# Moving the low parts of split f32 operands by 128 bytes in SBUF

## What is computed

```python
for l in range(2):                                   # first block
    z = rms_norm(x, norm_mix[l]) @ w_in[l]           # 1024 x 2560
    x = x + mix(z) @ w_out[l]                        # 1024 x 1024
    h = rms_norm(x, norm_mlp[l])
    x = x + square(relu(h @ w_mlp_in[l])) @ w_mlp_out[l]
for l in range(2):                                   # second block
    x = layer_norm(ALPHA * x + mix2(x, mem) @ w_out[l])
    h = einsum('td,thkd->thk', x, u[expert])         # u: 16384 x 1024
    x = layer_norm(ALPHA * x + einsum('thk,thkd->td', gelu(h) * gate, v[expert]))
```

## The kernel before

| tensor | before | after |
|---|---|---|
| `RAW`, `HI`, `HH`, `AH` | 128 | 128 |
| `LO`, `HL`, `AL` | 128 | 0 |
| `XH` | 64 | 64 |
| `XL` | 64 | 192 |
| `MEMH`, `MEML` | 128 | 0 |
| `G`, `RB`, `SQ`, `XS2`, first three `KVM` | 128 | 0 |

## Time and profile before

### The profile page before, as it was taken

How to read it: one execution, slowest core, us unless ns; L and a number is a source line. 1 busy time by engine, 2 the same in 40 slices (tenths; PEclk the granted TensorE clock), 3 DMA queues, 4 the chain that set the end, 5 groups by cost and what they waited for, 6 DMA issues and landing times.

```text
span 2731.0 us, 45677 instructions
## 1 busy us (share of the span) xinstructions
PE 2652.6 (97%) x18520; PEld 2418.1 (89%) x18520; DVE 1706.0 (62%) x2680; ACT 1373.5 (50%) x1713; POOL 191.1 (7%) x130
## 2 busy tenths in 40 slices
PE   8989999899999999999999999999999999999997
PEld 7869889699888999999999888988999999999886
DVE  5657446475455899655555666566899655555665
ACT  5555343654364569644444443444578634444442
POOL 0210000300001500000000000002400000000000
PEclk9999999999999999999999999999999999999999
DMA  5316552155535446756565675524356756556672
GB/s 219 109 66 218 197 204 94 62 204 199 189 113 194 152 165 237 278 202 225 203 215 206 240 267 194 189 78 156 140 181 242 280 195 224 207 211 219 227 268 86
DMA packets 74411, 515.99 MB, mean 189 GB/s; under 512 B 8272, under 2 KB 8544, under 8 KB 18592
## 3 DMA queue, kind: packets, MB, share of 16 engines
q1 hardware_dynamic: 58576, 424.70, 43.6%
q0 software_dynamic: 10208, 43.45, 4.5%
q10 hardware_dynamic: 5488, 45.91, 4.1%
HBM read 474.19 MB, written 39.85 MB: 188 GB/s over the span
## 4 chain that ended last, share of the span: by engine, by line
PE 87%; DVE 9%; ACT 2%; issue 1%; DMA 1%; POOL 1%; ACTq 0%; DVEq 0%; POOLq 0%
PE lin L1590 17%; PE lin L1592 17%; PE lin L1591 17%; PE m L1590 9%; PE m L1592 8%; PE m L1591 8%; PE m L2127 4%; DVE lo L958 1%; PE m L1709 1%; PE m L1730 1%; POOL w L1532 1%; PE m L2106 0%; PE m L2026 0%; PE lin L1764 0%; PE m L1742 0%
## 5 line engine op out<-in xcount | busy, mean ns | idle before, releaser
L958 DVE TENSOR_TENSOR lo<-raw,hi 128x2048 fp32r<-128x2048 f32 x357 | 817.8, 2296 | 652.9 <-ACT hi L448 651.8
L448 ACT ACTIVATE hi<-raw 128x2048 fp32r<-128x2048 f32 x403 | 769.7, 1913 | 479.8 <-PE m L1592 340.8
L1590 PE MATMUL lin<-xh,hi 128*128 128x256 f32 x3376 | 962.3, 285 | 16.2 <-DVE lo L958 9.0
L1591 PE MATMUL lin<-xl,hi 128*128 128x256 f32 x3376 | 943.3, 279 | 0.0
L1592 PE MATMUL lin<-xh,lo 128*128 128x256 f32 x3376 | 943.0, 279 | 0.0
L1590 PEld LDWEIGHTS lin<-xh,hi 128*128 128x128 f32 x3376 | 636.7, 189 | 24.9 <-DVE lo L958 10.2
L1592 PEld LDWEIGHTS lin<-xh,lo 128*128 128x128 f32 x3376 | 641.3, 190 | 0.0
L1591 PEld LDWEIGHTS lin<-xl,hi 128*128 128x128 f32 x3376 | 638.0, 189 | 3.6 <-issue 1.0
L1590 PE MATMUL m<-hi,ah 128*128 128x512 f32 x1024 | 398.8, 389 | 0.0
L1592 PE MATMUL m<-hi,al 128*128 128x512 f32 x1024 | 398.4, 389 | 0.0
L1591 PE MATMUL m<-lo,ah 128*128 128x512 f32 x1024 | 398.4, 389 | 0.0
(11 more groups left out here) (358 smaller groups left out, 2928.1 us busy)
## 6 DMA issues: line engine op xcount, KB each, us to landing
raw<-stream SPq DMA_DIRECT2D x403, 1024.0 KB, 4.8
gate_table<-stg ACTq DMA_DIRECT2D x16, 2048.0 KB, 10.9
g<-gate_table POOLq DMA_DIRECT2D x32, 1024.0 KB, 8.6
rows<-rows ACTq DMA_DIRECT2D x4, 1024.0 KB, 6.9
memh<-mem_turned_scratch POOLq DMA_DIRECT2D x3, 1024.0 KB, 5.1
meml<-mem_turned_scratch POOLq DMA_DIRECT2D x3, 1024.0 KB, 8.3
x_scratch<-x ACTq DMA_DIRECT2D x2, 1024.0 KB, 4.2
x<-x_scratch ACTq DMA_DIRECT2D x2, 1024.0 KB, 6.8
```

Source lines behind the costliest of these rows:

```text
L448: act.activation(HI[i % SLOTS][:], RAW[:, i % SLOTS, :], ACT.Copy).then_inc(hi_ready, 1)
L958: dve.tensor_tensor(LO[i % SLOTS][:], RAW[:, i % SLOTS, :], HI[i % SLOTS][:].bitcast(F32), ALU.subtract).then_inc(lo_ready, 1)
L1590: pe.matmul(out_, ah, bh, start=first, stop=False, **kw)
L1591: pe.matmul(out_, ah, bl, start=False, stop=False, **kw)
```

## The change

All low parts that take part in `three` are given a place 128 bytes off, modulo 256, from that of their high parts. For this `LOW = 128` is added ahead of `LO`, of `XL` and of `AL`, and to the offsets of `HL`; padding that stood in the cursor's way is lessened by the same amount, so that `XH` and `CST` and all behind them stay where they were. `MEMH` and `MEML` and some buffers that follow a shifted one move along. No instruction is added, removed or moved: on each engine the same instructions stand in the same order with the same waits, and only the addresses in them differ.

```diff
--- before.py
+++ after.py
@@ -14,6 +14,7 @@
 AX = mybir.AxisListType
 
 P = 128
+LOW = 128
 TOK = 256
 TT = TOK // P
 D = 1024
@@ -152,11 +153,12 @@
 
         RAW = at("raw", [P, SLOTS, HP])
         HI = [at(f"hi{i}", [P, HP], F32R) for i in range(SLOTS)]
+        cursor[0] += LOW
         LO = [at(f"lo{i}", [P, HP], F32R) for i in range(SLOTS)]
-        cursor[0] += 192
+        cursor[0] += 192 - LOW
         XH = at("xh", [P, KT, TOK], F32R)
+        cursor[0] += LOW
         XL = at("xl", [P, KT, TOK], F32R)
-        cursor[0] += 128
         cst0 = cursor[0]
         CST = at("cst", [P, N_CONST])
         SMALL = at("small", [P, 112])
@@ -198,16 +200,16 @@
         PM = at("pm", [P, 3, 2, TOK], off=r1)
         PT = at("pt", [P, 2, 2, TOK], off=r1 + 6144)
         MEMR = at("memr", [P, TT, D], off=mix0 + 8192)
-        MEMH = at("memh", [P, KT, TOK], F32R, off=mix0 + 40960)
-        MEML = at("meml", [P, KT, TOK], F32R, off=mix0 + 49152)
-        KVM = [at(f"kvm{i}", [P, 512], off=mix0 + (57344 if i < 3 else 8192)) for i in range(N_MEM)]
+        MEMH = at("memh", [P, KT, TOK], F32R, off=mix0 + 40960 + LOW)
+        MEML = at("meml", [P, KT, TOK], F32R, off=mix0 + 49152 + LOW)
+        KVM = [at(f"kvm{i}", [P, 512], off=mix0 + (57344 + LOW if i < 3 else 8192)) for i in range(N_MEM)]
 
         HH = at("hh", [P, 32, TOK], F32R, off=mix0)
-        HL = at("hl", [P, 32, TOK], F32R, off=mix0 + 32768)
-        RB = at("rb", [P, 2, 2 * TOK], off=mix0 + 65536)
-        SQ = at("sq", [P, 2 * TOK], off=mix0 + 65536 + 4096)
-        XS2 = at("xs2", [P, TT, D], off=mix0 + 65536)
-        assert mix0 + 65536 + 8192 <= top - 4 * LEVELS * 128
+        HL = at("hl", [P, 32, TOK], F32R, off=mix0 + 32768 + LOW)
+        RB = at("rb", [P, 2, 2 * TOK], off=mix0 + 65536 + LOW)
+        SQ = at("sq", [P, 2 * TOK], off=mix0 + 65536 + LOW + 4096)
+        XS2 = at("xs2", [P, TT, D], off=mix0 + 65536 + LOW)
+        assert mix0 + 65536 + LOW + 8192 <= top - 4 * LEVELS * 128
 
         def cst(name):
             a, b = CONST[name]
```

## The result

The changed kernel takes 2792.8 us (median of two runs, 2792.7 to 2792.9) against 2738.83: ratio 1.0185, 95% interval [1.0163, 1.0206]. It is slower. The forecast was 2736 with a range up to 2780; the result lies outside it and near rival C (2798).

A forecast was written before the change was run, and what follows sets the result against it. TensorE, 97% busy, was taken to bound the kernel through `three`'s products. Pairs 0 and `memh` -0.5 us took 2733.2 to 2732.7; with the runs' median 2738.8 and redrawn paces, 2736 was forecast, range 2706 to 2780.

The forecast's parts named there:

- rival C: TensorE triples: own weights or another neighbour's count, so two of three pairs change; 65 us slower, 2798; chance 0.11.
- every effect must be one of addresses: Whole kernel: the change moves no instruction, only start addresses, so only addresses can have an effect.
- The DVE row: DVE's low part `lo<-raw,hi`: expected within 20 ns of 2292; net cost taken as 0.
- and of no other: TensorE: only the next product's weights load beside a product, so only that pair's addresses can collide; the change keeps its distance.
- 3376 x 0 + 1280 x 0 = 0 us: Cost of the shifted pairs in 3376 triples of 256 columns and 1280 of 512: nothing, since each pair keeps its distance.
- this untested half: The claim that only the next product's weights matter, on which case A, no change in the pairs, rested; chance 0.76.
- 64 and 192 both occur now without harm at 256 columns: Argument against rival C: both distances modulo 256 between moving data and weights already occur in 256-column triples without harm.
- The two paces: 256-column triples run at 0.353 or 0.340 us; about 1650 of 3376 at the slow one, costing about 22 us.
- B: Rival: the slow pace of 256-column triples goes; 22 us faster (30 at the upper count), 2711; chance 0.08.
- If locks are drawn anew: 256-column stretches may lock into either pace afresh, 11 us either way, putting the next median between 2732.7 and 2738.8.
- D: Rival: the products' basic overhead goes at both widths; 80 us faster, 2653, or 104 us by the skill's formula, 2629; chance 0.05.
- a third pace: TensorE triples at a pace other than the known ones: listed as a sign of being wrong, without a price.

The follow-up runs named there:

- e7: The changed kernel with the second and third product of each triple exchanged, all addresses kept; ratio to the kernel before 1.0108, median 2772.1 us.
- m1: Kernel before, experts' product operands read beside their place in thirty-two settings, values wrong; only paces used: 256 columns 340 to 363 ns, 512 columns 680 to 701.
- W+X1: Setting in m1: product 3's weights and product 1's moving data 128 bytes further; 353 ns at 256 columns (base distance 192), 699 at 512 (base distance 0).
- e5: Kernel before with low parts 128 bytes further only for panels of 256-column triples, each low tile 128 bytes longer; ratio 0.9974, 2739.0 us beside 2745.4.

## Why the prediction was wrong, step by step

- "every effect must be one of addresses", and one of TensorE's products: right. The DVE row moved by 1 ns (forecast: within 20), no wait took a gap's place, `g`, `rb`, `sq`, `xs2` and `kvm` cost nothing that can be seen, and the products account for 57.9 of 59.5 us.
- The step that failed is in what bounds the kernel now: "beside product i the array loads the weights of product i+1, and of no other. That is the pair whose addresses can collide." The first half is what the timeline shows. "And of no other" is not, and it was to be seen in the row that I quoted: the load for L1592 starts at 1168.80 and lasts 0.19, to 1168.99, and its own product starts before that, as the next row of the same timeline says:

```profile
1168.91 0.28 PE L1592 MATMUL lin<-xh,lo 128*128 128x256 f32 x1
```

So at 256 columns each product is recorded beside the last 0.08 us of its own weights' load as well; I had looked at where the loads start and not at where they end. At 512 columns the records do not overlap (a load of 0.19 in a pace of 0.227), and w moved all the same, so this can't be the whole of it. The step fails by the runs whatever the cause: the change keeps each product's distance to the next one's weights, and c went to 363 and w to 693; e7 keeps the changed kernel's own distances, and 363 became 353. From that half-sentence came "3376 x 0 + 1280 x 0 = 0 us", which is +39.1 and +15.8 us in the trace.

- That no row of before could carry it was to be seen: there high and low lie alike in every triple, so a product's distances to its own weights, to the next one's and to those before it are the same number, and no row can tell which of them counts. On this untested half I put 0.76.
- Rival C named the kind of mechanism (own weights or a neighbour's) and priced it at 46 + 19 = 65 us; the trace has 39.1 + 15.8, and 3.0 more elsewhere. Its measuring sticks were nearly right as well: 0.360 from `memh` for what came to 0.363, and 0.695 for what came to 0.693. That they came so near is in part luck: 0.360 was read at distance 0 and 0.695 at 64, and those triples of the changed kernel have other distances. What was wrong was the argument "64 and 192 both occur now without harm at 256 columns". They do, one at a time and for whole triples: m1 has 353 at 64 and 340 or 353 at 192. One mixture of the two within a triple costs 363; the same three own distances as W+X1 has them cost 353.
- The two paces were right. So was their count, 1591 of the summed triples at 353 or 354 against my 1650, with some luck, since I had put it midway between 1124 and 2300. B's mechanism exists too, only not in this change: with `LO` alone moved the slow pace goes, and that is worth 15 us (1143.7 to 1128.4) where I had 22.
- "If locks are drawn anew" failed: in the changed kernel nothing is drawn, c is at 363 in every stage.
- D falls: no setting here took c below 340 or w below 680. The formula N/2.4 + 2.5 ns, from which I had a second price for it, stands in the Trainium skill's page "TensorE: Matmul & The Clock Gate", section "Back-to-back issue gap", for the isolated gap of one product, not for a row of loads and products.
- The text listed "a third pace" as what would prove it wrong without a price. That is what came.

The Trainium skill's page "TensorE: Matmul & The Clock Gate", section "Step-by-step: what each phase is for", says that moving data and weight loads have separate read ports and that a load takes no bandwidth from a running product. By that, as the prediction read it, no placement could matter. The runs disagree with this reading: equal instructions, and with e7 even equal addresses, pace 340 to 363 ns at 256 columns and 680 to 700 at 512.

What stays open is the rule behind the table. I found no sum of a price per distance that gives all 24 entries, which two or three distances count is not shown, the rhythm of five triples at 363 is unexplained, and so is what decides between 340 and 353 at a = 192. Whether the neighbour that matters is the next product or the one before can't be told from these runs, since with three products in a ring a change of one distance changes another.

## What to carry to other kernels

Where matmuls run back to back with a weight load each, read the pace from start to start and look at the places of all operands of neighbouring products modulo 256: here they were worth 0.7% one way and 1.9% the other with no instruction changed. Don't reason the best placement out: give every panel of one kernel another setting, read the paces off a single trace, and then place each kind of product by itself, since what is best for one (c wants the low weights 128 away) costs another (w wants them alike). And where a forecast of "nothing" rests on a quantity that the change keeps, ask what it does not keep, and which row has tested that.

## What the runs showed that I had not expected

- The order of two products that add to the same sum, at equal addresses, is worth 0.8% of the kernel (ratio 1.0185 to 1.0108): c goes from 363 to 353 ns, while w rises from 693 to 700.
- Two halves of a change can be worth nothing and +1.1%, and +1.85% together.
- The same operands modulo 256 can run at two steady paces (c at 340 and 353, w at 687 and 700); c held each of them for whole stages.
- A tile that is 128 bytes longer moves all that follow it: e5's slots alternated between two paces, panel by panel.
